# A mixed-layer block whose projections read their columns in permuted orders

## The chip, the cores and the metric

The kernel runs on one core of one Trainium2 chip. The metric is the device time of one execution, in microseconds (us); lower is better.

## The reference, cut to what matters

Four layers work on x (256 tokens x 2048 features, float32): an even layer (chunked attention and an mLSTM), an odd layer (an RG-LRU and a gated delta rule), then a layer with dilated and differential attention, a layer with 16 heads of block attention (at 256 tokens a causal attention over one block), and a last norm. For this change only one thing counts: each layer begins with a wide projection of the normed x and ends with one back to 2048 features that is added to x.

```python
proj = rmsnorm(x, norm_g) @ w_in
...
y = jnp.concatenate([ya, yb], axis=-1).astype(x.dtype)
return x + y @ w_out
```

## The kernel before, in words

Everything that is not one of these two products is work in small pieces that is fitted between the pieces of the projections by an order of steps made when the program is built.

*Jobs.* `job_list` cuts all projections into 104 jobs in the order in which they run. A job makes 512 output columns (256 in mode "wide", 8 or 16 for the two "few" jobs), summed over 16 k-tiles of 128 input features. Layer 0: va, qb, kb, gif, vb, qa, ka, za, ob, zb, out. Layer 1: qds, kds, ab, vd, qd, kd, vd, xcs, zd, zc, out. Layers 2 and 3: v0, q0, k0, q1, k1, v1, zs, zg, out. Each name stands for two jobs of 512 columns (numbered b = 0 and 1; in layer 1 qd and kd of b = 0 are wide, so the "feat" jobs are vd for b = 0 and 1, and qd and kd for b = 1), four or eight wide ones of 256 (qb, kb, qds, kds, xcs, q0 to k1; layer 0 has eight wide jobs, layer 3 sixteen), and four for out.

*Pieces.* `piece_list` cuts each job into pieces of 1024 float32 weights a partition: two k-tiles of 512 columns or four of 256. For every piece, SyncE's queue loads RAW (8 buffers in turn), ScalarE copies it to WH in fp32r (L1105; 6 buffers), which rounds it, and VectorE writes the remainder RAW - WH to WL in fp32r (L1474; 8 buffers). The activations are kept in the same way as a high and a low part, XHL with 16 k-tiles x (256 high, 256 low) columns for the in-projections, YHA/YHB and YLA/YLB for the out-projections. A product of two float32 matrices is then the sum of three fp32r products: high x high, high x low, low x high.

*Matmuls.* In the function `products` (on TensorE), the mode says which operand is held in the array and which one moves past it:

- "tok" (L743 to L745): 128 tokens of the activations are held, 512 columns of WH or WL move. Tokens come out in the partitions of the accumulator.
- "wide" (L748 to L751): 128 columns of weights are held; the 512 columns of XHL (256 tokens high, 256 tokens low), or the 256 high ones, move. VectorE adds the two halves afterwards (`halves_of`).
- "feat" (L756 to L758): 128 columns of weights are held, 256 tokens move.
- the first three pieces of va (L735 to L739) and the last four of the last job (L774 to L776) are written out on their own, with the reads of "tok".

Accumulators are ACC0 and ACC1 in turn, each of 1024 columns. ScalarE and VectorE read a finished one (`evacuate`) while the next job fills the other; job j waits until job j-2 has been read out. VectorE's sums of halves are L1482 (layer 0, qb and kb), L1504 (layer 1) and L1522 (layers 2 and 3, q and k). TensorE also does the small matmuls of the steps, for example L938, which sums squares with one-column matmuls.

`arrange`, on the host, writes the weights piece by piece into one array `w`, in the order in which they are loaded.

Of the kernel before, what the change touches and what calls it, by code (L numbers as in the profile page):

```python
# [10 lines left out]
ALU = mybir.AluOpType  # L11
# [69 lines left out]
def job_list():  # L81
    jobs = []
# [41 lines left out]
    for layer, w, wo, at in ((2, "w_in_ab_2", "w_out_ab_2", ((3072, 4096, 5120, 7168), (0, 1024, 2048, 6144))),  # L124
# [10 lines left out]
        out(layer, wo, (2, 3, 0, 1))  # L135
    return jobs


# [19 lines left out]
def program(nc, I, out):  # L158
    ctx = ExitStack()
    with ctx:  # L160
# [463 lines left out]
        def halves_of(j):  # L624

            return ACC[j % 2][:, :].rearrange("p (g h c) -> p g c h", g=2, h=2)

# [62 lines left out]
        def tensor(e):  # L690
# [8 lines left out]
            def products(p):  # L699
# [13 lines left out]
                for kk in range(nk):  # L713
# [17 lines left out]
                    elif p < EARLY:  # L731

                        e.wait_ge((s_hi0, s_hi)[kk], p + 1)
                        for t in range(2):
                            e.matmul(acc[t], xh[:, 128 * t:128 * t + 128], hi[:, kk, :], start=f, stop=False)  # L735
                            e.matmul(acc[t], xl[:, 128 * t:128 * t + 128], hi[:, kk, :], start=False, stop=False)
                        e.wait_ge((s_lo0, s_lo)[kk], p + 1)
                        for t in range(2):
                            m = e.matmul(acc[t], xh[:, 128 * t:128 * t + 128], lo[:, kk, :], start=False, stop=l)  # L739
                    elif J.mode == "tok":  # L740
                        for t in range(2):
                            th, tl, o = xh[:, 128 * t:128 * t + 128], xl[:, 128 * t:128 * t + 128], acc[t][:, 0:w]
                            e.matmul(o, th, hi[:, kk, :], start=f, stop=False)  # L743
                            e.matmul(o, th, lo[:, kk, :], start=False, stop=False)  # L744
                            m = e.matmul(o, tl, hi[:, kk, :], start=False, stop=l)  # L745
                    elif J.mode == "wide":
                        (wh0, wh1), (wl0, wl1) = ((w[:, kk, 0:128], w[:, kk, 128:256]) for w in (hi, lo))
                        e.matmul(acc[0], wh0, XHL3[:, kt, :], start=f, stop=False, skip_group_check=True)  # L748
                        e.matmul(acc[0][:, 0:256], wl0, xh, start=False, stop=l, skip_group_check=True)  # L749
                        e.matmul(acc[1][:, 0:256], wl1, xh, start=f, stop=False, skip_group_check=True)  # L750
                        m = e.matmul(acc[1], wh1, XHL3[:, kt, :], start=False, stop=l, skip_group_check=True)  # L751
                    else:
                        for g in range(w // 128):
                            o = acc[g // 2][:, 256 * (g % 2):256 * (g % 2) + 256]
                            wh, wl = hi[:, kk, 128 * g:128 * g + 128], lo[:, kk, 128 * g:128 * g + 128]
                            e.matmul(o, wh, xh, start=f and g % 2 == 0, stop=False, skip_group_check=True)  # L756
                            e.matmul(o, wh, xl, start=False, stop=False, skip_group_check=True)  # L757
                            m = e.matmul(o, wl, xh, start=False, stop=l, skip_group_check=True)  # L758
# [701 lines left out]
        def vector(e):  # L1460
# [15 lines left out]
            def evacuate(j, p):  # L1476
                J, acc = jobs[j], acc_of(j)
                c = slice(512 * J.b, 512 * J.b + 512)
                if J.kind == "feat":
                    f = two(S[0 if J.name == "qb" else 1][:, 512 * J.b:512 * J.b + 512])  # L1480
                    e.wait_ge(s_mm, p + 1)
                    e.tensor_reduce(f, halves_of(j), AX, ALU.add).then_inc(s_evD)  # L1482
                    e.wait_ge(s_row, 1)
# [31 lines left out]
                elif J.kind == "rope":  # L1515
# [5 lines left out]
                    e.wait_ge(s_mm, p + 1)  # L1521
                    e.tensor_reduce(dst, halves_of(j), AX, ALU.add).then_inc(s_evD)  # L1522
                    e.wait_ge(s_row, J.layer + 1)
# [596 lines left out]
def arrange(a):  # L2120
# [9 lines left out]
    for j, k0, nk in piece_list(jobs):  # L2130
        J = jobs[j]
        x = a[J.w][0][128 * k0:128 * (k0 + nk), J.c0:J.c0 + J.n]
        x = _np.ascontiguousarray(x.reshape(nk, 128, J.n).transpose(1, 0, 2).reshape(128, nk * J.n))
# [50 lines left out]
```

## Time and profile before

| what | value |
|---|---|
| median of 2 runs | 1908.26 us (1908.25 to 1908.27) |
| profiled execution | 1909.72 us, span from first to last instruction 1907.8 us |
| TensorE busy | 1897.6 us of the span |
| VectorE, ScalarE, GpSimd busy | 1217.3, 1011.0, 167.4 us |
| moved by DMA | 340.28 MB, 178 GB/s |
| mean granted TensorE clock | 0.998 |

The lines L of the profile are those of the kernel before. PE is TensorE's matmuls, PEld its weight loads (they overlap the matmuls), DVE is VectorE, ACT ScalarE, POOL GpSimd, SP SyncE. Matmuls overlap each other too, so the time between two starts is their pace, and the duration of one is more than that.

### The profile page before, as it was taken

What the parts mean: (1) busy time and instruction counts of PE and PEld (TensorE: products, weight loads), DVE (VectorE), ACT (ScalarE), POOL (GpSimd) and SP (SyncE); (2) the same over time, 40 slices, a digit from 0 to 9 for tenths busy, and PEclk for the clock granted to TensorE, in tenths of its full rate; (3) what the DMA queues carried; (4) which work ended last, traced back from release to release, by engine and by line L of the source; (5) the groups of instructions that cost most, each with busy time, mean ns of one, the idle gap of its engine ahead of it and who ended that gap; (6) DMA issues with size and microseconds to landing.
All of it is one profiled execution on the core that took longest, in us unless ns stands there. A gap on an engine that the chain in (4) does not pass through costs nothing.

```text
span 1907.8 us, 26779 instructions
## 1 busy us (share of the span) xinstructions
PE 1897.6 (99%) x10658; PEld 1630.6 (85%) x10658; DVE 1217.3 (64%) x1682; ACT 1011.0 (53%) x1572; POOL 167.4 (9%) x142
## 2 busy tenths in 40 slices
PE   9999999999999999999999999999999999999998
PEld 7888888888889998898888888888888888888886
DVE  6654655554566787687557888645555778844553
ACT  7434445664556765765543344556454344445643
POOL 0000000110011101100001211000000111100110
PEclk9999999999999999999999999999999999999999
DMA  9555545545554444444565555554555555455453
GB/s 350 191 182 180 176 164 182 174 167 178 182 175 165 155 148 159 151 164 159 183 198 188 189 177 166 191 169 164 177 182 189 189 186 170 166 187 170 162 198 133
DMA packets 95035, 340.28 MB, mean 178 GB/s; under 512 B 10704, under 2 KB 11472, under 8 KB 94784
## 3 DMA queue, kind: packets, MB, share of 16 engines
q1 hardware_dynamic: 93536, 333.92, 52.0%
q0 software_dynamic: 944, 3.61, 0.6%
q8 instruction: 85, 1.39, 0.3%
q10 hardware_dynamic: 432, 1.06, 0.1%
q14 instruction: 38, 0.31, 0.1%
HBM read 336.44 MB, written 2.10 MB: 177 GB/s over the span
## 4 chain that ended last, share of the span: by engine, by line
PE 99%; DMA 0%; SPq 0%; ACT 0%; DVE 0%; issue 0%
PE ACC L743 18%; PE ACC L745 18%; PE ACC L744 18%; PE ACC L748 9%; PE ACC L751 9%; PE ACC L750 5%; PE ACC L749 5%; PE ACC L756 2%; PE ACC L757 2%; PE ACC L758 2%; PE PM L859 1%; PE PM L874 1%; PE PM L912 1%; PE PM L896 1%; PE PM L897 1%; PE PM L895 1%
## 5 line engine op out<-in xcount | busy, mean ns | idle before, releaser
L1474 DVE TENSOR_TENSOR WL<-RAW,WH 128x1024 fp32r<-128x1024 f32 (+1 forms) x624 | 792.0, 1285 | 531.2 <-ACT WH L1105 529.4
L1105 ACT ACTIVATE WH<-RAW 128x1024 fp32r<-128x1024 f32 (+1 forms) x626 | 650.7, 1052 | 506.2 <-PE ACC L745 263.4
L743 PE MATMUL ACC<-WH,XHL 128*128 128x512 f32 x1012 | 402.4, 398 | 0.3 <-DVE WL L1474 0.3
L745 PE MATMUL ACC<-WH,XHL 128*128 128x512 f32 x1012 | 394.4, 390 | 0.0
L744 PE MATMUL ACC<-WL,XHL 128*128 128x512 f32 x1012 | 394.0, 389 | 0.0
L748 PE MATMUL ACC<-XHL,WH 128*128 128x512 f32 x768 | 308.5, 402 | 0.0
L751 PE MATMUL ACC<-XHL,WH 128*128 128x512 f32 x768 | 304.3, 396 | 0.0
L745 PEld LDWEIGHTS ACC<-WH,XHL 128*128 128x128 f32 x1012 | 189.9, 188 | 40.2
L743 PEld LDWEIGHTS ACC<-WH,XHL 128*128 128x128 f32 x1012 | 190.1, 188 | 39.0 <-DVE WL L1474 0.7
L744 PEld LDWEIGHTS ACC<-WL,XHL 128*128 128x128 f32 x1012 | 190.1, 188 | 38.6
L750 PE MATMUL ACC<-XHL,WL 128*128 128x256 f32 x768 | 214.2, 279 | 0.0
L749 PE MATMUL ACC<-XHL,WL 128*128 128x256 f32 x768 | 213.6, 278 | 0.0
L750 PEld LDWEIGHTS ACC<-XHL,WL 128*128 128x128 f32 x768 | 144.6, 188 | 35.2
L749 PEld LDWEIGHTS ACC<-XHL,WL 128*128 128x128 f32 x768 | 144.9, 189 | 32.4
L748 PEld LDWEIGHTS ACC<-XHL,WH 128*128 128x128 f32 x768 | 146.0, 190 | 0.9
L751 PEld LDWEIGHTS ACC<-XHL,WH 128*128 128x128 f32 x768 | 144.3, 188 | 0.0
L756 PE MATMUL ACC<-XHL,WH 128*128 128x256 f32 x384 | 110.5, 288 | 0.0
L2020 POOL TENSOR_TENSOR S<-S 128x512 f32<-128x512 f32 x32 | 67.0, 2092 | 479.6 <-DVE S L1530 479.6
L757 PE MATMUL ACC<-XHL,WH 128*128 128x256 f32 x384 | 108.6, 283 | 0.0
L758 PE MATMUL ACC<-XHL,WL 128*128 128x256 f32 x384 | 108.6, 283 | 0.0
L743 PE MATMUL ACC<-WH,YHB 128*128 128x512 f32 x256 | 101.1, 395 | 0.0
L745 PE MATMUL ACC<-WH,YLB 128*128 128x512 f32 x256 | 99.8, 390 | 0.0
(374 smaller groups left out, 2339.9 us busy)
## 6 DMA issues: line engine op xcount, KB each, us to landing
RAW<-in_w SPq DMA_DIRECT2D x621, 512.0 KB, 3.3
X<-in_x SPq DMA_DIRECT2D x4, 512.0 KB, 11.9
RAW<-in_w SPq DMA_DIRECT2D x6, 256.0 KB, 4.5
Y<-in_xT SPq DMA_DIRECT2D x2, 512.0 KB, 11.3
S<-in_bias POOLq DMA_DIRECT2D x8, 128.0 KB, 2.7
S<-in_od_gate_w POOLq DMA_DIRECT2D x1, 1024.0 KB, 5.8
S<-in_final_norm POOLq DMA_DIRECT2D x1, 1024.0 KB, 7.9
out<-Y SPq DMA_DIRECT2D x2, 512.0 KB, 2.6
```

The lines of the kernel that those rows point to most:

```text
L743: e.matmul(o, th, hi[:, kk, :], start=f, stop=False)
L744: e.matmul(o, th, lo[:, kk, :], start=False, stop=False)
L745: m = e.matmul(o, tl, hi[:, kk, :], start=False, stop=l)
L748: e.matmul(acc[0], wh0, XHL3[:, kt, :], start=f, stop=False, skip_group_check=True)
L749: e.matmul(acc[0][:, 0:256], wl0, xh, start=False, stop=l, skip_group_check=True)
L750: e.matmul(acc[1][:, 0:256], wl1, xh, start=f, stop=False, skip_group_check=True)
L751: m = e.matmul(acc[1], wh1, XHL3[:, kt, :], start=False, stop=l, skip_group_check=True)
L756: e.matmul(o, wh, xh, start=f and g % 2 == 0, stop=False, skip_group_check=True)
L757: e.matmul(o, wh, xl, start=False, stop=False, skip_group_check=True)
L758: m = e.matmul(o, wl, xh, start=False, stop=l, skip_group_check=True)
L1105: e.activation(hi, src, ACT.Copy).then_inc(s_hi)
L1474: e.tensor_tensor(lo, src, hi.bitcast(F32), ALU.subtract).then_inc(s_lo)
```

## The change: what it does

Each projection job listed in `READ` has its weights permuted by the host within each k-tile (`read_order`), and TensorE reads the moving weights through a view (`read_view`) that undoes the permutation. The numbers are columns of 4 bytes.

- `halves(512, run=r, apart=d)` reads r columns at one place, r at a place d further on, and so on in turn; without `apart` d is 256. One-column runs are read at distances 256 (va, layer 0's out), 128 (qa, layer 3's v0), 64 (zd), 32 (layer 1's out), 16 (layer 2's v0), 8 (layer 2's v1), 4 (layer 2's out) and 2 (layer 2's zs). Runs of 2, 4 and 8 columns at distance 256 are read in ka, za and ob.
- `("c a", "a c", ...)` reads every a-th column, and comes back for the rest: steps of 2 (zb), 4 (layer 2's zg) and 16 (layer 3's v1).
- vb is read in its old order, by an address pattern of two dimensions.
- Layer 0's wide jobs read the activations' columns in turn at 128 columns' distance (token c and token c + 128). Layer 3's wide jobs read two high columns, two low ones, and so on (distance 256); there the accumulator is in that order too, so the products with the low weights write pairs of columns with gaps of two.
- In layer 1, zc loads weights with every fourth column, and kd (b = 1) with every second.
- VectorE's sums of halves in layers 0 and 3 take their operands in the new order.

Layer 3's zs, zg and out, layer 1's and 2's wide jobs and the reads of the activations in "feat" jobs are as before.

```diff
--- before.py
+++ after.py
@@ -134,6 +134,48 @@
         both(layer, "zg", w, at[0][3], "tok", "gate")
         out(layer, wo, (2, 3, 0, 1))
     return jobs
+
+
+def halves(width, run=1, apart=None):
+
+    apart = apart or width // 2
+    return "g a c r", "g c a r", {"g": width // (2 * apart), "a": 2, "c": apart // run, "r": run}
+
+
+READ = {(0, "va"): halves(512), (0, "vb"): ("c r", "c r", {"c": 256, "r": 2}), (0, "qa"): halves(512, apart=128),
+        (0, "ka"): halves(512, run=2), (0, "za"): halves(512, run=4), (0, "ob"): halves(512, run=8),
+        (0, "zb"): ("c a", "a c", {"a": 2, "c": 256}), (0, "out"): halves(512),
+        (1, "zd"): halves(512, apart=64), (1, "out"): halves(512, apart=32),
+        (2, "v0"): halves(512, apart=16), (2, "v1"): halves(512, apart=8), (2, "zs"): halves(512, apart=2),
+        (2, "zg"): ("c a", "a c", {"a": 4, "c": 128}), (2, "out"): halves(512, apart=4),
+        (3, "v0"): halves(512, apart=128), (3, "v1"): ("c a", "a c", {"a": 16, "c": 32})}
+LOAD = {(1, "zc"): 4, (1, "kd"): 2}
+
+
+def read_order(how):
+
+    if how is None:
+        return slice(None)
+    mem, read, n = how
+    mem, read = mem.split(), read.split()
+    at = np.arange(int(np.prod([n[x] for x in mem]))).reshape([n[x] for x in mem])
+    return at.transpose([mem.index(x) for x in read]).ravel()
+
+
+def load_at(J, g):
+
+    n = LOAD.get((J.layer, J.name), 1)
+    at = 128 * n * (g // n) + g % n
+    return slice(at, at + 128 * n - (n - 1), n)
+
+
+def read_view(x, how):
+
+    if how is None:
+        return x
+    mem, read, n = how
+    keep = [a for a in mem.split() if n[a] > 1]
+    return x.rearrange(f"p ({' '.join(keep)}) -> p {' '.join(a for a in read.split() if n[a] > 1)}", **{a: n[a] for a in keep})
 
 
 def piece_list(jobs):
@@ -623,6 +665,10 @@
 
         def halves_of(j):
 
+            if jobs[j].layer == 0:
+                return ACC[j % 2][:, :].rearrange("p (g h c t) -> p g t c h", g=2, h=2, t=2)
+            if jobs[j].layer == 3:
+                return ACC[j % 2][:, :].rearrange("p (c h r) -> p c r h", h=2, r=2)
             return ACC[j % 2][:, :].rearrange("p (g h c) -> p g c h", g=2, h=2)
 
         x_rows = I["x"].rearrange("(t p) c -> p t c", p=128)
@@ -732,17 +778,34 @@
 
                         e.wait_ge((s_hi0, s_hi)[kk], p + 1)
                         for t in range(2):
-                            e.matmul(acc[t], xh[:, 128 * t:128 * t + 128], hi[:, kk, :], start=f, stop=False)
-                            e.matmul(acc[t], xl[:, 128 * t:128 * t + 128], hi[:, kk, :], start=False, stop=False)
+                            e.matmul(acc[t], xh[:, 128 * t:128 * t + 128], read_view(hi[:, kk, :], READ[0, "va"]), start=f, stop=False)
+                            e.matmul(acc[t], xl[:, 128 * t:128 * t + 128], read_view(hi[:, kk, :], READ[0, "va"]), start=False, stop=False)
                         e.wait_ge((s_lo0, s_lo)[kk], p + 1)
                         for t in range(2):
-                            m = e.matmul(acc[t], xh[:, 128 * t:128 * t + 128], lo[:, kk, :], start=False, stop=l)
+                            m = e.matmul(acc[t], xh[:, 128 * t:128 * t + 128], read_view(lo[:, kk, :], READ[0, "va"]), start=False, stop=l)
                     elif J.mode == "tok":
+                        wh, wl = (read_view(x[:, kk, :], READ.get((J.layer, J.name))) for x in (hi, lo))
                         for t in range(2):
                             th, tl, o = xh[:, 128 * t:128 * t + 128], xl[:, 128 * t:128 * t + 128], acc[t][:, 0:w]
-                            e.matmul(o, th, hi[:, kk, :], start=f, stop=False)
-                            e.matmul(o, th, lo[:, kk, :], start=False, stop=False)
-                            m = e.matmul(o, tl, hi[:, kk, :], start=False, stop=l)
+                            e.matmul(o, th, wh, start=f, stop=False)
+                            e.matmul(o, th, wl, start=False, stop=False)
+                            m = e.matmul(o, tl, wh, start=False, stop=l)
+                    elif J.mode == "wide" and J.layer == 0:
+                        (wh0, wh1), (wl0, wl1) = ((w[:, kk, 0:128], w[:, kk, 128:256]) for w in (hi, lo))
+                        both = XHL3[:, kt, :].rearrange("p (h t c) -> p h c t", h=2, t=2)
+                        high = xh.rearrange("p (t c) -> p c t", t=2)
+                        e.matmul(acc[0], wh0, both, start=f, stop=False, skip_group_check=True)
+                        e.matmul(acc[0][:, 0:256], wl0, high, start=False, stop=l, skip_group_check=True)
+                        e.matmul(acc[1][:, 0:256], wl1, high, start=f, stop=False, skip_group_check=True)
+                        m = e.matmul(acc[1], wh1, both, start=False, stop=l, skip_group_check=True)
+                    elif J.mode == "wide" and J.layer == 3:
+                        (wh0, wh1), (wl0, wl1) = ((w[:, kk, 0:128], w[:, kk, 128:256]) for w in (hi, lo))
+                        both = XHL3[:, kt, :].rearrange("p (h c r) -> p c h r", h=2, r=2)
+                        high = [a.rearrange("p (c h r) -> p c h r", h=2, r=2)[:, :, 0, :] for a in acc]
+                        e.matmul(acc[0], wh0, both, start=f, stop=False, skip_group_check=True)
+                        e.matmul(high[0], wl0, xh, start=False, stop=l, skip_group_check=True)
+                        e.matmul(high[1], wl1, xh, start=f, stop=False, skip_group_check=True)
+                        m = e.matmul(acc[1], wh1, both, start=False, stop=l, skip_group_check=True)
                     elif J.mode == "wide":
                         (wh0, wh1), (wl0, wl1) = ((w[:, kk, 0:128], w[:, kk, 128:256]) for w in (hi, lo))
                         e.matmul(acc[0], wh0, XHL3[:, kt, :], start=f, stop=False, skip_group_check=True)
@@ -752,7 +815,7 @@
                     else:
                         for g in range(w // 128):
                             o = acc[g // 2][:, 256 * (g % 2):256 * (g % 2) + 256]
-                            wh, wl = hi[:, kk, 128 * g:128 * g + 128], lo[:, kk, 128 * g:128 * g + 128]
+                            wh, wl = (x[:, kk, load_at(J, g)] for x in (hi, lo))
                             e.matmul(o, wh, xh, start=f and g % 2 == 0, stop=False, skip_group_check=True)
                             e.matmul(o, wh, xl, start=False, stop=False, skip_group_check=True)
                             m = e.matmul(o, wl, xh, start=False, stop=l, skip_group_check=True)
@@ -1479,7 +1542,7 @@
                 if J.kind == "feat":
                     f = two(S[0 if J.name == "qb" else 1][:, 512 * J.b:512 * J.b + 512])
                     e.wait_ge(s_mm, p + 1)
-                    e.tensor_reduce(f, halves_of(j), AX, ALU.add).then_inc(s_evD)
+                    e.tensor_reduce(f.rearrange("p g (t c) -> p g t c", t=2), halves_of(j), AX, ALU.add).then_inc(s_evD)
                     e.wait_ge(s_row, 1)
                     e.wait_ge(s_evD, D_AT[j] - 1)
                     e.tensor_tensor(f, f, row2, ALU.mult).then_inc(s_evD)
@@ -1519,7 +1582,8 @@
                     lo, hi = slice(0, 64), slice(64, 128)
                     dst, t2 = feat(s)[:, 2 * J.b:2 * J.b + 2, :], two(S6[:, 512 * (r % 2):512 * (r % 2) + 512])
                     e.wait_ge(s_mm, p + 1)
-                    e.tensor_reduce(dst, halves_of(j), AX, ALU.add).then_inc(s_evD)
+                    summed = S[s][:, 512 * J.b:512 * J.b + 512].rearrange("p (c r) -> p c r", r=2) if J.layer == 3 else dst
+                    e.tensor_reduce(summed, halves_of(j), AX, ALU.add).then_inc(s_evD)
                     e.wait_ge(s_row, J.layer + 1)
                     if r > 1:
                         e.wait_ge(s_rot, r - 1)
@@ -2129,7 +2193,13 @@
     jobs = job_list()
     for j, k0, nk in piece_list(jobs):
         J = jobs[j]
-        x = a[J.w][0][128 * k0:128 * (k0 + nk), J.c0:J.c0 + J.n]
+        w = a[J.w][0][128 * k0:128 * (k0 + nk), J.c0:J.c0 + J.n]
+        x = _np.empty_like(w)
+        if J.mode == "tok":
+            x[:, read_order(READ.get((J.layer, J.name)) if J.n == 512 else None)] = w
+        else:
+            for g in range(J.n // 128):
+                x[:, load_at(J, g)] = w[:, 128 * g:128 * g + 128]
         x = _np.ascontiguousarray(x.reshape(nk, 128, J.n).transpose(1, 0, 2).reshape(128, nk * J.n))
         if nk == 16:
             m[f"few{J.layer}"] = x
```

## Rows read from the trace of the kernel before

**Rows 1.** The page: span, part 1 (busy us), part 2 (40 slices).

```profile
span 1907.8 us, 26779 instructions
...
PE 1897.6 (99%) x10658; PEld 1630.6 (85%) x10658; DVE 1217.3 (64%) x1682; ACT 1011.0 (53%) x1572; POOL 167.4 (9%) x142
...
PE   9999999999999999999999999999999999999998
...
PEclk9999999999999999999999999999999999999999
```

**Rows 2.** The page, part 4: the chain that ended last, shares of the span.

```profile
PE 99%; DMA 0%; SPq 0%; ACT 0%; DVE 0%; issue 0%
PE ACC L743 18%; PE ACC L745 18%; PE ACC L744 18%; PE ACC L748 9%; PE ACC L751 9%; PE ACC L750 5%; PE ACC L749 5%; PE ACC L756 2%; PE ACC L757 2%; PE ACC L758 2%; PE PM L859 1%; PE PM L874 1%; PE PM L912 1%; PE PM L896 1%; PE PM L897 1%; PE PM L895 1%
```

**Rows 3.** Groups by shape: xcount | busy us, mean ns | idle before.

```profile
L743 PE MATMUL ACC<-WH,XHL 128*128 128x512 f32 x1012 | 402.4, 398 | 0.3 <-DVE WL L1474 0.3
L745 PE MATMUL ACC<-WH,XHL 128*128 128x512 f32 x1012 | 394.4, 390 | 0.0
...
L748 PE MATMUL ACC<-XHL,WH 128*128 128x512 f32 x768 | 308.5, 402 | 0.0
...
L756 PE MATMUL ACC<-XHL,WH 128*128 128x256 f32 x384 | 110.5, 288 | 0.0
...
L756 PEld LDWEIGHTS ACC<-XHL,WH 128*128 128x128 f32 x384 | 73.6, 192 | 0.4
```

**Rows 4.** Timeline of TensorE in a "tok" job: start us, us, line.

```profile
438.84 0.39 PE L743 MATMUL ACC<-WH,YHB 128*128 128x512 f32 x1
...
439.52 0.39 PE L743 MATMUL ACC<-WH,YHB 128*128 128x512 f32 x1
```

**Rows 5.** Timeline of TensorE in a "feat" job: first and fourth start.

```profile
819.83 0.28 PE L757 MATMUL ACC<-XHL,WH 128*128 128x256 f32 x1
...
820.19 0.28 PE L757 MATMUL ACC<-XHL,WH 128*128 128x256 f32 x1
```

**Rows 6.** Groups by shape on VectorE: subtraction of splits, sums of halves.

```profile
L1474 DVE TENSOR_TENSOR WL<-RAW,WH 128x1024 fp32r<-128x1024 f32 x621 | 789.9, 1288 | 530.7 <-ACT WH L1105 528.9
...
L1522 DVE TENSOR_REDUCE S<-ACC 128x512 f32<-128x1024 f32 x32 | 39.1, 1222 | 7.9 <-PE ACC L751 7.7
...
L1482 DVE TENSOR_REDUCE S<-ACC 128x512 f32<-128x1024 f32 x8 | 9.8, 1224 | 4.9 <-PE ACC L751 4.9
```

**Rows 7.** Timeline of TensorE: sixteen one-column matmuls, each with a weight load.

```profile
604.70 1.84 PE L938 MATMUL PM<-C,S 128*128 128x1 f32 x16
606.41 0.36 PE L756 MATMUL ACC<-XHL,WH 128*128 128x256 f32 x1
```

**Rows 8.** Windows: busy us of each engine, clock, DMA share, GB/s.

```profile
438.80:460.80 22.00, 22.00 (x107) 18.36 (x107) 11.80 (x11) 11.11 (x15) 3.42 (x3) 1.00 0.51 171
20.00:64.00 44.00, 44.00 (x213) 37.01 (x212) 29.34 (x36) 30.16 (x47) 1.50 (x4) 1.00 0.80 304
```

**Rows 9.** Timeline of TensorE at the start, same columns as in rows 4.

```profile
22.35 0.39 PE L744 MATMUL ACC<-WL,XHL 128*128 128x512 f32 x1
...
23.03 0.39 PE L744 MATMUL ACC<-WL,XHL 128*128 128x512 f32 x1
```

**Rows 10.** Timeline of TensorE in a wide job (four products, then the next).

```profile
99.89 0.39 PE L748 MATMUL ACC<-XHL,WH 128*128 128x512 f32 x1
100.12 0.28 PE L749 MATMUL ACC<-XHL,WL 128*128 128x256 f32 x1
100.24 0.28 PE L750 MATMUL ACC<-XHL,WL 128*128 128x256 f32 x1
100.36 0.40 PE L751 MATMUL ACC<-XHL,WH 128*128 128x512 f32 x1
100.59 0.40 PE L748 MATMUL ACC<-XHL,WH 128*128 128x512 f32 x1
```

## The prediction

> **What bounds the kernel now.** I read the first part of the page first: TensorE is busy for 1897.6 of 1907.8 us, and no other engine above 64% [rows 1]. The chain of work that ended last says the same from the other end: 99% of it is TensorE, and its largest terms are the projection lines L743 to L758 [rows 2]. Then the groups of instructions: the idle time ahead of TensorE's projection groups is 0.3 us at most, so no wait for weights, splits or evacuation is left on the path [rows 3]. So what the change does to DVE, ACT or the DMAs matters only if it is large, and what it does to the pace of a matmul counts in full. A busy time of a matmul (398 ns) overlaps with the next one's, so the pace has to be read from starts in the timeline: 439.52 less 438.84 over three matmuls of 512 columns is 0.227 us each [rows 4]; 256-column matmuls of the "feat" branch start (820.19 - 819.83)/3 = 0.120 apart [rows 5]. The second 256 columns therefore cost 0.107 us, 512 columns cost 0.213, and some 0.014 of each matmul is fixed. That is 2.4 columns per ns, which is the higher of the clock's two levels (2.4 GHz), and the page shows the granted clock at nine tenths or more in every slice [rows 1].
>
> **What the change leaves alone.** It adds and removes no matmul, no column, no byte of DMA and no wait. The weights come from HBM already permuted, in the same contiguous pieces; the split of ACT and DVE is elementwise on whole pieces; what reaches the accumulators of the "tok" branch is again in the old order. These edits have one answer, zero. What differs is the addresses from which TensorE reads, at one place where it writes, and those from which DVE sums.
>
> **Moving operand, counted.** A "tok" job has 16 k-tiles x 2 token halves x 3 products = 96 matmuls of 512 columns. I sort the orders by how many neighbouring columns lie together.
> - One column, then a jump to a place at 4 to 256 columns' distance, and back: va 2 jobs, qa 2, the outs of layers 0, 1 and 2 4 each, zd 2, layer 2's v0 and v1 2 each, layer 3's v0 2: 24 jobs. One column, then on by 4 or 16, never back: layer 2's zg and layer 3's v1, 4 jobs. Together 28 x 96 = 2688 matmuls.
> - Layer 0's eight wide jobs read the activations in turn at 128 columns' distance: 8 x 16 x 2 = 256 matmuls of 512 columns, and as many of 256. That is worth 384 of 512 columns. With the above: 3072.
> - Two or more columns close together: ka (runs of 2), za (4), ob (8), zb (steps of 2), zs (places 2 apart), layer 3's sixteen wide jobs (runs of 2). vb only has its address written in two dimensions. The rest (layer 1's wide and "feat" reads of the activations, layer 2's wide, layer 3's zs, zg and out) is read as before.
>
> **What such a read costs.** No TensorE row of this trace reads a moving operand with a jump inside it, so the price is bounded from the nearest rows.
> Below: nothing. DVE's sum of two halves (L1522, L1482) reads 1024 elements of PSUM in turn from two places 256 columns apart in 1222 ns, while its subtraction of 1024 contiguous elements takes 1288 [rows 6]. So a reading engine of this chip jumps on every element without losing any time, but at 0.8 elements per ns (1024 in 1222), a third of TensorE's pace. No row gives a reason for a gain, so the lower end is zero.
> Above: the fastest stream of separately addressed columns that is not a moving operand is the weight load. Sixteen pairs of a load and a one-column matmul take 604.70 to 606.41, so 1.71/16 = 107 ns for 128 columns, 1.2 per ns [rows 7]. At that pace 512 columns take 428 ns, 0.215 more than the 0.213 of now. At DVE's pace they would take 512 x 1222/1024 = 611 ns, 0.40 more. I take the weight load's: it is TensorE's own read of the same memory, and the rate nearest to the one asked for. The thought behind it is that a memory that has to deliver a new place every 0.42 ns is asked for more than any row here shows, while with two columns at a place the same rate asks for 1.2 places per ns, which the loads show. So I price one-column orders at double streaming time and the others at nothing.
> The sum: 3072 x 0.213 = 655 us. On the profiled execution (1909.7 us, span 1907.8) [rows 1] that makes 2565; on the median of 1908.3 it makes 2563. If the fixed 0.014 hides behind the slower stream, the sum is 3072 x (0.428 - 0.227) = 617, or 2525. I write 2560.
>
> The Trainium skill speaks to this: "SBUF — State Buffer", under "Door 1: The DMA port swizzle", states 16-byte lines, of which at least two hits in a row are needed for full bandwidth; with 4-byte elements a stride of up to four elements would be mild and one column per line would pay. It names no price for a matmul, and no run so far shows one. By its words the jumps of 2 (zs, zb) and runs of 2 are free.
>
> **Strided weights.** zc loads every fourth column (2 jobs x 192 = 384 loads), layer 1's kd every second (192). A load takes 192 ns by its row, latency included [rows 3], 107 by the pace above, beside a matmul whose step is 120 [rows 5]: the cover is thin. Lower end 0; if a load of separate places takes double, the step becomes about 0.227 and zc costs 384 x 0.107 = 41 us. I take 0, since 107 ns for 128 columns is already the pace that I ascribe to separate places.
>
> **Writes and sums.** In layer 3's wide jobs the low products (16 x 16 x 2 = 512 matmuls of 256 columns) write PSUM in runs of two with gaps of two. No row shows a gapped write of this size; between 0 and a doubling, 512 x 0.107 = 55 us. I take 0, by the same reasoning on pairs.
> A sentence of the same skill speaks against that choice: "PSUM — Partial Sum Buffer", in its "Specifications (TRN2)", says that any non-contiguous pattern slows matmuls significantly, with 8-byte lines.
> DVE's sums in layers 0 and 3 keep their element count; even at twice 1222 ns, 24 of them add 29 us to an engine that is idle for a third of the span, and each has a whole next job (11 us or more) before its accumulator is wanted again: zero, and about 1 us per job if that cover were gone. As TensorE slows, ACT's and DVE's releases come later but so do their uses; no new wait appears, and loads land earlier relative to use.
>
> **Rivals.**
> - *Nothing happens*, 1908 us. The moving operand is fetched ahead with enough parallelism that order is irrelevant. For it: DVE's free jumps [rows 6], and a pace of matmuls that is the same 0.227 while DMAs move 304 GB/s as while they move 171 (22.35 to 23.03 over three matmuls) [rows 4, 8, 9]. Against it: the threefold rate. It decides if the pace of a one-column job in the timeline stays at 0.227. This is the case in which the kernel isn't slower.
> - *Only places never returned to cost*: the reader keeps both alternating places open. Then zg and layer 3's v1 alone pay, 4 x 96 x 0.213 = 82 us: 1991.
> - *Distance decides*: near places lie in different parts of the memory and are read side by side, far ones clash. With the line between 32 and 64 columns: va, qa, out of layer 0, zd, layer 3's v0 (12 jobs, 1152) and the wide 384: 1536 x 0.213 = 328: 2236; other lines between 2000 and 2500.
> - *Pairs pay too*: ka, zb, zs (576) and layer 3's wide reads (512) double also: 1088 x 0.213 = 232 more, 2795.
>
> **How the numbers follow.** Double streaming of one-column orders 0.50 (its own range 2500 to 2650: the hidden fixed part below, zc's 41 us and layer 3's 55 above); nothing 0.30; never returned 0.07; distance 0.09; pairs too 0.04. The forecast is 2560. To hold 8 in 10 the range must reach the second case, so it runs from 1900 to 2650, with only the last rival and a price beyond double outside. The runs of now agree to 0.02 us, so 2% (38 us) is a bound well above their scatter: slower by over 2% is everything but the second case, 0.69 with a little off for a gain from nowhere; within 2% 0.30; faster 0.01.
>
> **What would show it.** In the timeline of the changed kernel: starts 0.43 to 0.44 apart in va, qa, zd, zg and the outs of layers 0 to 2; 0.227 in vb, za, ob and, by my sorting, in ka, zb and zs; well over the 0.69 to 0.70 of now [rows 10] for the four products of layer 3's wide jobs would mean that pairs pay (1.12 by the doubling of its two reads of 512); a step above 0.12 in zc means the load. The prediction is wrong if the one-column jobs keep 0.227, or if they split by distance, and its size is wrong if the pace settles anywhere else than near that of the weight load. A granted clock at its lower level (1.2 GHz) in those jobs would be a different cause with a similar size.

## The result and the profile after

The changed kernel takes 2129.2 us against 1908.3: the ratio is 1.116, with a 95% interval of 1.113 to 1.119. It is slower by 221 us, where 652 had been forecast.

The page of the changed kernel, parts 1, 2 and 4. It answers to [rows 1] and [rows 2]; in the new file the tok products are L790 to L792, layer 0's wide ones L797 to L800, layer 3's L805 to L808, the other wide ones L811 to L814, feat L819 to L821.

```profile
span 2127.2 us, 26779 instructions
...
PE 2114.8 (99%) x10658; PEld 1695.0 (80%) x10658; DVE 1217.8 (57%) x1682; ACT 1012.0 (48%) x1572; POOL 165.8 (8%) x142
...
PE   9999999999999999999999999999999999999998
...
PEclk9999999999999999999999999999999999999999
...
PE 98%; DMA 1%; ACT 1%; DVE 0%; issue 0%; SPq 0%; ACTq 0%
```

TensorE is busy for 99% of the span as before, at the same granted clock, and VectorE and ScalarE work as long as before (1217.8 and 1012.0 us). TensorE's idle time grows only from 10.2 to 12.4 us. So nearly all of the 221 us are in the pace of the matmuls: each matmul of some jobs takes longer.

The timeline of TensorE shows the pace job by job. Its first column is the start in us; the difference of two starts is what counts. The first stretch is va (one column in turn, 256 apart), then ka (two columns in turn, 256 apart), za (four), zb (every second column), layer 2's zg (every fourth), zc (256-column products, weights loaded by every fourth column) and one of layer 3's wide jobs (two columns in turn; four products from one start to the next).

```profile
30.21 0.38 PE L790 MATMUL ACC<-WH,XHL 128*128 128x512 f32 x1
...
30.85 0.38 PE L790 MATMUL ACC<-WH,XHL 128*128 128x512 f32 x1
...
256.62 0.51 PE L792 MATMUL ACC<-WH,XHL 128*128 128x512 f32 x1
...
257.61 0.51 PE L792 MATMUL ACC<-WH,XHL 128*128 128x512 f32 x1
...
320.04 0.42 PE L792 MATMUL ACC<-WH,XHL 128*128 128x512 f32 x1
...
320.79 0.41 PE L792 MATMUL ACC<-WH,XHL 128*128 128x512 f32 x1
...
429.68 0.63 PE L790 MATMUL ACC<-WH,XHL 128*128 128x512 f32 x1
...
431.04 0.63 PE L790 MATMUL ACC<-WH,XHL 128*128 128x512 f32 x1
...
1399.73 0.66 PE L791 MATMUL ACC<-WL,XHL 128*128 128x512 f32 x1
...
1401.12 0.66 PE L791 MATMUL ACC<-WL,XHL 128*128 128x512 f32 x1
...
879.79 0.40 PE L821 MATMUL ACC<-XHL,WL 128*128 128x256 f32 x1
...
880.49 0.40 PE L821 MATMUL ACC<-XHL,WL 128*128 128x256 f32 x1
...
1630.66 0.50 PE L805 MATMUL ACC<-XHL,WH 128*128 128x512 f32 x1
...
1631.57 0.50 PE L805 MATMUL ACC<-XHL,WH 128*128 128x512 f32 x1
```

Three matmuls each: 0.64 in va, 0.99 in ka, 0.75 in za, 1.36 in zb, 1.39 in zg, 0.70 in zc. Before it was 0.68 [rows 4] and in the feat jobs 0.36 [rows 5]. The four products of the wide job take 0.91, before 0.70 [rows 10]. So va is not slower but *faster* than contiguous reading, zb has doubled although its columns lie in pairs within 16 bytes, and zc has doubled although only its weight loads changed.

A start is shown to 0.01 us, so the paces below are worked out from starts twelve matmuls apart, and what stands is the lowest fifth of a job's values, which leaves out the places where a small step comes between (for wide jobs the median over sixteen): 0.2267 for a contiguous tok job (512 columns at 2.4 per ns take 0.2133, and 0.0134 is a fixed part), 0.2158 for every job of one-column turns, whether at 256, 128, 64, 32, 16, 8 or 4 columns' distance (fixed part 0.0025).

| job of the changed kernel | order | pace before, us | after, us | matmuls | sum, us |
|---|---|---|---|---|---|
| 24 tok jobs | one column in turn, distance 4 to 256 | 0.2267 | 0.2158 | 2304 | -25.1 |
| layer 0's wide | one column in turn, 128 | 0.1742 (mean of four) | 0.1638 | 512 | -5.3 |
| ka | runs of 2, distance 256 | 0.2267 | 0.3283 and 0.3333 | 192 | +20.0 |
| za, ob | runs of 4, of 8 | 0.2267 | 0.2500, 0.2433 | 384 | +7.7 |
| zb, zg of layer 2, v1 of layer 3 | steps of 2, 4, 16 | 0.2267 | 0.451, 0.461, 0.433 | 576 | +127.7 |
| layer 3's wide | runs of 2, distance 256; half of them write with gaps | 0.1742 (mean of four) | 0.2250 | 1024 | +52.0 |
| zc | weights by steps of 4 | 0.1200 | 0.2333 | 384 | +43.5 |
| zs (distance 2), vb, kd | | | as before | | 0 |
| all | | | | | +220.5 |

The sum of the paces explains the measured 221 us without any wait. vb, whose address has two dimensions but the old order, keeps 0.2267: a second dimension in the address costs nothing by itself.

That the clock did not do this is seen in the windows of zb, layer 3's v1 and zc (busy us of each engine, then the granted clock, DMA share and GB/s):

```profile
416.00:440.00 24.00, 24.00 (x67) 12.06 (x66) 6.37 (x9) 7.36 (x15) 0.84 (x2) 1.00 0.25 89
1862.00:1880.00 18.00, 18.00 (x47) 8.93 (x46) 4.13 (x4) 3.69 (x5) 0.00 (x0) 1.00 0.31 102
870.00:890.00 20.00, 20.00 (x87) 20.00 (x87) 9.58 (x21) 9.44 (x15) 0.00 (x0) 1.00 0.28 83
```

The clock is at 1.00, the higher level, in all three. The DMAs' rate is 83 to 102 GB/s in these stretches; over the whole kernel the bytes moved are the same 340.28 MB as before, spread over a longer time.

### The profile page after: what moved, and what is told of

Its sections match the earlier page's. It is cut to its first block, busy times and chain, and to the rows that moved or that the text cites. A ratio compares the mean times of both kernels' runs of the same rounds, so it can differ in the third digit from the quotient of the medians.

```text
span 2127.2 us, 26779 instructions
## 1 busy us (share of the span) xinstructions
PE 2114.8 (99%) x10658; PEld 1695.0 (80%) x10658; DVE 1217.8 (57%) x1682; ACT 1012.0 (48%) x1572; POOL 165.8 (8%) x142
## 2 busy tenths in 40 slices
DMA packets 95035, 340.28 MB, mean 160 GB/s; under 512 B 10704, under 2 KB 11472, under 8 KB 94784
## 3 DMA queue, kind: packets, MB, share of 16 engines
q8 instruction: 85, 1.39, 0.3%
## 4 chain that ended last, share of the span: by engine, by line
PE 98%; DMA 1%; ACT 1%; DVE 0%; issue 0%; SPq 0%; ACTq 0%
PE ACC L790 18%; PE ACC L792 18%; PE ACC L791 18%; PE ACC L811 4%; PE ACC L814 4%; PE ACC L808 4%; PE ACC L805 4%; PE ACC L819 3%; PE ACC L820 3%; PE ACC L821 3%; PE ACC L813 2%; PE ACC L812 2%; PE ACC L807 2%; PE ACC L806 1%; PE ACC L800 1%; PE ACC L797 1%
## 5 line engine op out<-in xcount | busy, mean ns | idle before, releaser
L790 PE MATMUL ACC<-WH,XHL 128*128 128x512 f32 x1012 | 455.4, 450 | 0.5 <-DVE WL L1537 0.5
L792 PE MATMUL ACC<-WH,XHL 128*128 128x512 f32 x1012 | 447.8, 443 | 0.0
L791 PE MATMUL ACC<-WL,XHL 128*128 128x512 f32 x1012 | 447.8, 442 | 0.0
L792 PEld LDWEIGHTS ACC<-WH,XHL 128*128 128x128 f32 x1012 | 195.0, 193 | 82.3 <-issue 46.3
L790 PEld LDWEIGHTS ACC<-WH,XHL 128*128 128x128 f32 x1012 | 194.8, 192 | 78.6 <-issue 42.1
L791 PEld LDWEIGHTS ACC<-WL,XHL 128*128 128x128 f32 x1012 | 194.8, 193 | 77.8 <-issue 42.9
L811 PE MATMUL ACC<-XHL,WH 128*128 128x512 f32 x384 | 154.4, 402 | 0.0
L814 PE MATMUL ACC<-XHL,WH 128*128 128x512 f32 x384 | 151.9, 396 | 0.0
L805 PE MATMUL ACC<-XHL,WH 128*128 128x512 f32 x256 | 129.7, 507 | 0.0
L808 PE MATMUL ACC<-XHL,WH 128*128 128x512 f32 x256 | 126.3, 494 | 0.0
L819 PE MATMUL ACC<-XHL,WH 128*128 128x256 f32 x384 | 124.9, 325 | 0.0
L821 PE MATMUL ACC<-XHL,WL 128*128 128x256 f32 x384 | 123.0, 320 | 0.0
L820 PE MATMUL ACC<-XHL,WH 128*128 128x256 f32 x384 | 123.0, 320 | 0.0
L813 PE MATMUL ACC<-XHL,WL 128*128 128x256 f32 x384 | 106.9, 278 | 0.0
L812 PE MATMUL ACC<-XHL,WL 128*128 128x256 f32 x384 | 106.6, 278 | 0.0
L790 PE MATMUL ACC<-WH,YHB 128*128 128x512 f32 x256 | 99.0, 387 | 0.0
L792 PE MATMUL ACC<-WH,YLB 128*128 128x512 f32 x256 | 97.7, 382 | 0.0
L791 PE MATMUL ACC<-WL,YHB 128*128 128x512 f32 x256 | 97.7, 382 | 0.0
L790 PE MATMUL ACC<-WH,YHA 128*128 128x512 f32 x240 | 92.5, 385 | 0.0
```

Of the source, the lines that this page charges most:

```text
L790: e.matmul(o, th, wh, start=f, stop=False)
L791: e.matmul(o, th, wl, start=False, stop=False)
L792: m = e.matmul(o, tl, wh, start=False, stop=l)
L805: e.matmul(acc[0], wh0, both, start=f, stop=False, skip_group_check=True)
L808: m = e.matmul(acc[1], wh1, both, start=False, stop=l, skip_group_check=True)
```

## The experiments

**Only the turns.** The kernel before with the one-column turns of the change alone (`WIDE` names the layers whose wide jobs read the activations in turn):

```diff
-READ = {...}
+READ = {(0, "va"): halves(512), (0, "qa"): halves(512, apart=128), (0, "out"): halves(512), (1, "zd"): halves(512, apart=64),
+        (1, "out"): halves(512, apart=32), (2, "v0"): halves(512, apart=16), (2, "v1"): halves(512, apart=8),
+        (2, "out"): halves(512, apart=4), (3, "v0"): halves(512, apart=128)}
+WIDE = {0: "turn"}
```

> Only the one-column turns of the change: va, qa, zd, the outs of layers 0 to 2, v0 and v1 of layer 2, v0 of layer 3 (24 tok jobs, distances 4 to 256) and layer 0's eight wide jobs; everything else as in the kernel before. The prediction priced these at (24 x 96 + 384) x 0.213 = 573 us more, 2481. The theory after the result (each is 0.0109 or 0.0107 us a matmul shorter): 2304 x 0.0109 + 512 x 0.0107 = 31 us less, 1877.

Measured: 1878.2 us, ratio 0.984 (0.983 to 0.986): 30 us *faster* than the kernel before, and within 1 us of the sum of paces. This is the part on which nearly all of the forecast rested, and its sign was wrong.

**Only the steps.** The reads and loads by steps alone:

```diff
-READ = {...}
+READ = {(0, "zb"): ("c a", "a c", {"a": 2, "c": 256}), (2, "zg"): ("c a", "a c", {"a": 4, "c": 128}),
+        (3, "v1"): ("c a", "a c", {"a": 16, "c": 32})}
 LOAD = {(1, "zc"): 4, (1, "kd"): 2}
```

> Only the steps of the change: zb reads every 2nd column, layer 2's zg every 4th, layer 3's v1 every 16th, zc and kd load weights by 4 and 2; all else as before. The theory after the result: 192 matmuls each at 0.451, 0.461 and 0.433 instead of 0.227, so 43 + 45 + 40 us, and zc 384 x 0.113 = 43.5, together 171 and 2079 us. By the prediction zb, zc and kd cost nothing, and zg and v1 82 us: 1990. If part of the loss is made up because splits and small steps run ahead during slow jobs, less than 2079.

Measured: 2079.3 us in one run. The 171 us are all on the path; nothing is made up elsewhere.

**Weight loads undone.** The changed kernel with zc's and kd's loads contiguous again:

```diff
-LOAD = {(1, "zc"): 4, (1, "kd"): 2}
+LOAD = {}
```

> The changed kernel with its weight loads (zc, kd) contiguous again, all reads of moving operands as changed. Theory path: zc's 384 matmuls go back from 0.233 to 0.120, 43.5 us off, 2086 us; kd changes nothing. Rival: part of that time comes back as waits in the out jobs of layer 1 that follow, 2100 to 2129.

Measured: 2085.8 us in one run, 43 less than the changed kernel, as the path theory had it; zc's pace is 0.1200 again. kd's pace is 0.1200 with steps of 2 and without. The cover that the prediction called thin doesn't hold at all at steps of 4: the load is then the longer of the two and sets the step.

**A sweep of orders.** Thirty tok jobs, each with an order of its own (three of them here); the whole took 2290.6 us in one run:

```diff
+        (0, 'out', 2): ("h c s", "s c h", {"h": 2, "c": 128, "s": 2}),   # a0 b0 a2 b2 a4 b4 ...
+        (0, 'zb', 0): ("a c", "c a", {"a": 4, "c": 128}),                # four places in turn
+        (0, 'zb', 1): ("a c", "c a", {"a": 8, "c": 64}),                 # eight
```

> Each tok job of layers 0 to 2 reads in another order; wide, feat and layer 3 as in the kernel before. Paces of a 512-column matmul. Theory two readers: even-numbered and odd-numbered columns of the read order go through a reader each, a step takes one column of each (0.83 ns), each reader keeps its last 16-byte piece (4 columns) and can take another only every second step. It says 0.227 or less for runs of 16 to 128 in two places, for the crossed order a0 b0 a2 b2 (each reader then moves by steps of 2 in its own place), and 0.44 for 4 or more places in turn, for pairs with gaps (0 1 4 5), for steps of 4 to 64. Theory one store: both readers share a store of several pieces: 4 (perhaps 8 or 16) places in turn run at 0.216, and the crossed order costs 0.44, since it needs a new piece at each step. Theory jumps: the price goes by the number of jumps further than a piece, falling as 2, 4, 8 (0.333, 0.250, 0.243 in the changed kernel), 16, 32; it cannot say why one-column turns are free.

The timeline of the sweep kernel in the crossed order (layer 0's third out job), in four and in eight places in turn:

```profile
680.02 0.39 PE L845 MATMUL ACC<-WH,YHB 128*128 128x512 f32 x1
...
680.71 0.39 PE L845 MATMUL ACC<-WH,YHB 128*128 128x512 f32 x1
...
509.59 0.45 PE L845 MATMUL ACC<-WH,XHL 128*128 128x512 f32 x1
...
510.44 0.45 PE L845 MATMUL ACC<-WH,XHL 128*128 128x512 f32 x1
...
544.75 0.69 PE L851 MATMUL ACC<-WH,XHL 128*128 128x512 f32 x1
...
546.21 0.69 PE L851 MATMUL ACC<-WH,XHL 128*128 128x512 f32 x1
```

0.69 for three matmuls of the crossed order, 0.85 for four places, 1.46 for eight. All paces of this kernel, with those of the changed one that belong beside them:

| order | pace, us |
|---|---|
| one column in turn, two places | 0.2158 |
| the same at distance 2; crossed a0 b0 a2 b2 | 0.2267 |
| crossed by 4 (a0 b0 a4 b4) | 0.451 |
| steps of 2, 4, 8, 16, 32, 64 | 0.451, 0.461, 0.431, 0.433, 0.435, 0.487 |
| pairs with gaps of two (0 1 4 5) | 0.451 |
| four places in turn, 128 apart, 16, 4 | 0.283, 0.269, 0.268 |
| 8, 16, 32, 64, 128 places in turn | 0.487, 0.446, 0.433, 0.432, 0.435 |
| runs of 2 in 2, 4, 8, 32, 64 places | 0.333, 0.443, 0.487, 0.431, 0.460 |
| runs of 4 in 2, 4, 8 places | 0.250, 0.268, 0.276 |
| runs of 8 in 2, 4 places | 0.243, 0.231 |
| runs of 16, 32, 64, 128 in two places | 0.240, 0.237, 0.227, 0.227 |

What follows. The theory of one shared store falls: it wants 0.44 for the crossed order, and that runs like contiguous columns. The theory of jumps falls with it, and with the one-column turns. The theory of two readers holds for the crossed order, the gapped pairs and, within some 10%, the steps. It errs on four places in turn, for which it said 0.44, and on runs of 16 and 32 columns, for which it said 0.227 or less and which take 0.240 and 0.237. With one more clause it covers four places in turn as well: each reader keeps *two* pieces of 16 bytes. One of them can be filled ahead while the other is read; if both are in use in turn, the filling can't be hidden. Four places in turn then cost two extra steps (of 0.833 ns, two columns) in every eight, 1.25 x 0.2133 = 0.267 and a fixed part, so 0.269 to 0.280; runs of 2 in two places cost two in four, 0.320 and 0.0134 = 0.333; eight places are more than two pieces a reader and cost double. That clause was formed on these numbers, except for the check below. It gives no reason why runs of 4 to 32 stay above 0.2267, nor why steps of 64 and eight places take 0.487 where 0.44 was expected.

**Loads, fixed part, and more orders.** The kernel before with other weight loads, with smaller ones, and with more orders (in `LOAD` the first number is the step between the columns of a load; `SMALL` says how many tokens are loaded; the new orders of `READ` aren't shown):

```diff
+FEAT = {(1, 'vd', 0): 'turn', (1, 'qd', 1): 'turn', (1, 'zc', 0): 'turn'}
+LOAD = {(1, 'vd', 0): (4, None),
+        (1, 'vd', 1): (4, None),
+        (1, 'qd', 1): (2, None),
+        (1, 'kd', 1): (2, None)}
+SMALL = {(0, 'ka', 0): 32, (0, 'ka', 1): 64, (2, 'v0', 1): 32, (2, 'v1', 1): 32, (0, 'za', 0): 96, (2, 'v0', 0): 32}
...
+if (J.layer, J.name, J.b) in SMALL and not l:
+    n = SMALL[J.layer, J.name, J.b]
+    e.matmul(o[0:n, :], th[:, 0:n], wl, start=False, stop=False)
+    m = e.matmul(o[0:n, :], tl[:, 0:n], wh, start=False, stop=l)
+    continue
```

> As the kernel before, except: layer 1's feat jobs load weights by steps (vd 4, kd and qd 2, zc 1), vd 0, qd and zc 0 with the tokens in turn; in six jobs (layer 0's ka and za 0, layer 2's v0 and v1 1) two of three products load only 32, 64 or 96 of the 128 tokens, outside the last k-tile, so the low corrections of the other tokens are left out; nine jobs read runs or places in new ways. Weight load: one reader that takes a column a step (0.83 ns) and a new piece every second step says 0.233 for both vd jobs, in turn or not (128 x 2 steps = 213 ns, the load is the bound), and no loss for steps of 2 (0.120 contiguous, 0.112 in turn). The fixed 0.0134 us of a contiguous matmul, 0.0025 in turn: theory traffic (contiguous readers take a piece at every chance; the next weight load takes chances from them) says it falls with the load's size: ka 0 and v0 1 (32 tokens) to 0.221, ka 1 (64) to 0.223, za 0 (96) to 0.225. Theory start (a contiguous stream can't catch up a late start, whatever is loaded) says 0.2267 in all; in-turn ones stay at 0.216 by both. Runs of 4: if the distance of the jump costs (0.250 at 256 columns), gaps of 4 (vb 0) and 64 places 8 apart (qa 0) return to 0.227; if any step to a piece not the next does, they stay at 0.25. Four places in turn (0.283 at 128 columns, 0.268 at 4 and 16): two pieces kept per reader and two extra steps a round say 0.27 to 0.28 in ob 0 and 1 (32, 8 apart).

The timeline of this kernel: vd 0 (weights by steps of 4, tokens in turn), zc 0 (tokens in turn, weights contiguous), ka 0 (two of three products load 32 tokens), zb 1 (runs of 8 in 16 places, 32 apart); then a weight load of vd 0 (steps of 4) and one of kd (steps of 2).

```profile
599.95 0.40 PE L864 MATMUL ACC<-XHL,WH 128*128 128x256 f32 x1
...
600.65 0.40 PE L864 MATMUL ACC<-XHL,WH 128*128 128x256 f32 x1
...
869.83 0.28 PE L864 MATMUL ACC<-XHL,WH 128*128 128x256 f32 x1
...
870.17 0.28 PE L864 MATMUL ACC<-XHL,WH 128*128 128x256 f32 x1
...
261.80 0.39 PE L829 MATMUL ACC<-WH,XHL 128*128 128x512 f32 x1
...
262.48 0.39 PE L829 MATMUL ACC<-WH,XHL 128*128 128x512 f32 x1
...
437.25 0.38 PE L829 MATMUL ACC<-WH,XHL 128*128 128x512 f32 x1
...
437.91 0.38 PE L829 MATMUL ACC<-WH,XHL 128*128 128x512 f32 x1
```

```profile
599.82 0.33 PEld L864 LDWEIGHTS ACC<-XHL,WH 128*128 128x128 f32 x1
...
680.03 0.20 PEld L865 LDWEIGHTS ACC<-XHL,WH 128*128 128x128 f32 x1
```

The whole took 1966.9 us in one run. Both vd jobs run at 0.2333, in turn or not: the load sets this step. Its own row is longer too, 0.33 us against 0.20 in kd. The 0.2333 is what was expected beforehand if a column of the load takes 1.67 ns instead of 0.83, as for one reader that can take a new piece only every second step. Steps of 2 keep kd at 0.1200; but qd, with its tokens in turn, stays at 0.1200 too, where 0.112 was expected, while zc 0 with contiguous loads reaches 0.1117. So a load by steps of 2 isn't quite free, it only fits.

The fixed part: jobs with 32, 64 and 96 tokens loaded run at 0.230, 0.229 and 0.232, not below 0.2267. The traffic theory, that the load steals reading chances in proportion to its size, falls. The in-turn job with 32 tokens stays at 0.2158. The start theory said 0.2267 for all; the measured paces lie 3 to 5.5 ns above it, so it isn't shown either.

Runs of 4: with gaps of 4, and in 64 places 8 apart, 0.2333; in 16 places 32 apart 0.247; in two places 256 apart 0.250. Both answers on record were too simple: a part goes with the distance and a part (0.007) does not. Runs of 8 with gaps of 8 (vb 1) take 0.232. Runs of 8 in 16 places 32 apart (zb 1) take 0.220, less than contiguous columns: 0.66 over three in the lines above. None of the theories says so. Four places in turn at 32 and 8 apart: 0.273 and 0.269, as the two pieces with two extra steps a round had said beforehand.

**Everything in turn.** If one-column turns shorten the fixed part, they should be used everywhere, in every tok job (the last one included) and every wide one:

```diff
+READ = {"tok": halves(512)}
+WIDE = {0: "turn", 1: "turn", 2: "turn", 3: "turn"}
```

> All tok jobs read their weights one column in turn from two places 256 apart, all wide jobs read the activations in turn at 128; feat jobs and weight loads as in the kernel before. Theory A (the turn itself shortens each matmul's fixed part, from 0.0134 us to 0.0025 as the in-turn jobs of the changed kernel show at every distance from 4 to 256): 4608 tok matmuls x 0.0109 and 3072 wide ones x 0.0107 = 83 us off, 1825 us. Rival B (the shorter pace belongs to those jobs' surroundings, DMA and VectorE being less busy while other jobs are slow): no pace below 0.22 here, 1900 to 1908. Rival C (ScalarE's and VectorE's splits become the bound at the faster pace): between 1840 and 1908, with idle time of TensorE before VectorE's WL.

Measured: 1827.6 us, ratio 0.957 (0.956 to 0.959). The groups by shape, which answer to [rows 3], of this kernel (the tok products are L816, L817 and L822, wide L827 to L830, feat L850 to L852), and two starts of an out job:

```profile
L816 PE MATMUL ACC<-WH,XHL 128*128 128x512 f32 x1012 | 391.6, 387 | 0.5 <-DVE WL L1573 0.5
...
L822 PE MATMUL ACC<-WH,XHL 128*128 128x512 f32 x1012 | 383.5, 379 | 0.0
L827 PE MATMUL ACC<-XHL,WH 128*128 128x512 f32 x768 | 295.5, 385 | 1.2 <-DVE S L1592 1.2
...
L850 PE MATMUL ACC<-XHL,WH 128*128 128x256 f32 x384 | 110.5, 288 | 0.8 <-DVE S L1604 0.8
```

```profile
1750.71 0.38 PE L816 MATMUL ACC<-WH,YHB 128*128 128x512 f32 x1
...
1751.36 0.38 PE L816 MATMUL ACC<-WH,YHB 128*128 128x512 f32 x1
```

A matmul of L816 is shorter by 11 ns in the mean than L743 was (387 for 398), the pace is 0.65 over three, and its idle time before the groups shown is 1.2 us at most: ScalarE and VectorE keep up, so rival C falls, and rival B with the out job's pace.

The same with the feat jobs' tokens in turn as well:

```diff
+FEAT = {"feat": "turn"}
...
+mh, ml = (x.rearrange("p (t c) -> p c t", t=2) if feat_of(J) == "turn" else x for x in (xh, xl))
```

ScalarE's copies and VectorE's product of these accumulators then read them back in token order.

> As turn_all, and the feat jobs read their 256 tokens in turn at 128 as well. Theory A: 1152 matmuls go from 0.120 to 0.109, another 12 us off, 1812. Rival L (a weight load takes 107 ns and cannot start early, so feat is held by loads, not by the reads): feat stays at 0.120 and the time stays that of turn_all.

Measured: 1821.8 us, ratio 0.955 (0.953 to 0.957), the fastest of these kernels. feat's pace is 0.1117 (before 0.1200), not the 0.109 of theory A. It is near the 0.107 at which loads follow each other in [rows 7], so the load is probably what remains there, as rival L said of the bound though not of the size; no run isolates it. Of 1152 x 0.0083 = 9.6 us some 6 arrived. The traces show where the rest went: the feat jobs are shorter by 9.5 us, but layer 1's xcs jobs are longer by 2.2 and its out jobs by 1.0. In the first xcs job the granted clock is at its lower level for 3.4 us (windows of this kernel, before the fall and in it):

```profile
660.00:664.00 4.00, 4.00 (x91) 3.81 (x90) 3.97 (x5) 3.97 (x8) 1.92 (x1) 1.00 0.36 128
664.60:668.00 3.40, 3.40 (x12) 2.97 (x12) 3.40 (x8) 2.32 (x3) 0.00 (x0) 0.50 0.00 0
```

TensorE was busy all through both. The profiled execution of the kernel before has such a stretch too, at 695.8 us in the same job (granted clock 0.50 for 3.4 us), those of the changed kernel and of the kernel with all turns have none there. Why it falls there stays open.

## Why the prediction was wrong, point by point

- *What bounds the kernel.* Right: the change of the time is the change of the paces of TensorE's matmuls, 220 of 221 us. TensorE's idle time grew by 2.2 us only.
- *What such a read costs.* This is the step that failed. It priced a one-column order by the rate of "separately addressed columns" of the weight loads, as if every jump were a new access. It summed 3072 x 0.213 = 655 us. Measured, the 2688 of these that are turns (in columns of 512) gave 30 us back, and only the 384 of zg and layer 3's v1 cost what was said: 84.6 us for 82. The rate was near what steps cost (428 ns for 512 columns; 431 to 461 by steps), but that is luck: the loads of [rows 7] read contiguous columns, and a load of columns four apart runs at half that rate (0.2333 for zc). What was wrong besides is *which* orders come under it. A jump by itself costs nothing, since a turn jumps at every column; by the model of the sweep, which is inferred from the paces, what costs is a piece of 16 bytes that one reader has not got.
- "No row gives a reason for a gain, so the lower end is zero." Also wrong: the rows showed a fixed part of 0.014 us on each matmul [rows 4, 5], and I never asked what it was. Four fifths of it go with the order of the reads.
- *Two or more columns close together cost nothing.* Wrong for zb (43.1 us), ka (20.0), layer 3's wide jobs (52.0), za and ob (7.7); right for vb and zs. The rival "pairs pay too" named ka, zb, zs and the wide reads at 232 us; they cost 115, but it had them on top of the turns.
- *Strided weights.* The upper bound of 41 us was it: 43.5. The reason for taking 0, that 107 ns already is the pace of separate places, was wrong: 107 ns is the pace of contiguous columns, and the step with columns four apart is 0.2333, about twice the step of before.
- *Gapped writes* were nearly rightly taken as nothing: from the start of one of layer 3's 256-column products to the next start it is 0.124 us in the changed kernel, in layer 2 0.115 (means), 8 to 9 ns more, 4 to 5 us for 512. No run has the gapped writes without the pair reads around them, so the two aren't separated. The sums on VectorE cost nothing either.
- *Rivals.* None of them came true. The two with least chance were nearest: reading that keeps both alternating places ("only places never returned to cost") and pairs that pay. Each held half of the mechanism, and their sum (zg and v1, and the pairs), without the turns, would have given 1991 + 232 = 2223.
- *The scatter* of 0.02 us was that of two runs. Later runs of the kernel before lie between 1907.7 and 1910.1 us, a scatter still far below the 221.

The Trainium skill's "SBUF — State Buffer", under "Door 1: The DMA port swizzle", was read as "two columns in a row in a piece are enough". The measurements decide against that reading. The model of two readers agrees with its 16 bytes and its two hits if the hits are counted per reader, each of which sees every second column: zb hits each piece twice in a row and doubles, while kd's load, one column at a time, hits it twice and keeps 0.1200. Its sister page "PSUM — Partial Sum Buffer", in its "Specifications (TRN2)", says of non-contiguous patterns that they slow matmuls significantly; here products that write in pairs with gaps of two take 8 to 9 ns more than 115.

## What to carry to other kernels

Where TensorE reads its moving operand in float32r, try a layout in which two places, 4 to 256 columns apart, are read in turn, one column each: it took 10 to 11 ns off each of 7680 matmuls here, 4.3% of the time, for a permutation on the host and a three-dimensional address. Don't step over columns of 4 bytes in a moving operand, not even by two: every step tried, from 2 to 64, about doubled the time of a matmul. Weights loaded by steps of two stayed hidden beside 256-column matmuls, those loaded by steps of four did not. Other types were not tried. Before pricing an unknown access, ask how often each unit that reads would have to change its piece, and look for a fixed part in the pace of today that the change may touch.

## What the runs showed that I had not expected

- Contiguous reading is not the fastest: 0.2267 us for 512 columns against 0.2158 in one-column turns, at distances from 4 to 256 alike. The Trainium skill's "TensorE: Matmul & The Clock Gate", in "Back-to-back issue gap", gives N / 2.4 + 2.5 ns for a matmul by itself: for N = 512 that makes 0.2158, an estimate from its figures, and of the orders tried only one-column turns reach it. For a stream of matmuls with weight loads the same section gives 131 ns; no run here comes near it. In the model it goes with how often a reader must change its piece: the crossed order and distance 2, which change as often as contiguous columns do, are at 0.2267. But runs of 8 in 16 places, which change as often too, take 0.220. Why contiguous reading costs 11 ns once per matmul, and more rather than less with smaller weight loads, stays open.
- A model of two readers, each taking every second column, each with two pieces of 16 bytes and able to fetch one in two steps of 0.833 ns, gives, within some 10%, the paces of turns, steps, crossed orders, gapped pairs, four places and runs of two. It doesn't give what runs of 4 to 32 columns in several places take beyond 0.2267 (up to 0.05 us), nor the 0.220 of one of them, nor the spread from 0.431 to 0.487 of the orders at double time. It is inferred from paces alone.
